# A decoder layer's last stage: a root and a scaling earlier, one addition on GpSimd, sixteen transposes half a product later

## The chip, the cores and the metric

The kernel runs on one core of a Trainium2 chip. The metric is the device time of one execution in microseconds. TensorE multiplies matrices, VectorE, ScalarE and GpSimd work on elements, and SyncE (and ScalarE) issue the transfers. The engines run their own instruction lists and meet at semaphores.

## The reference, cut to what matters

One layer over 1024 tokens of width 1024, all in float32: an RMS norm, one input projection to 8720 columns, a sliding-window attention (16 heads) and an mLSTM (8 heads) side by side, a projection of each branch, a gated merge, an output projection with the residual, and a final RMS norm.

```
branch_a = (attn * silu(a_z)) @ w_branch_attn
h_m      = sigmoid(m_o) * head_rms_norm(h_tilde) * silu(m_z)
branch_m = h_m @ w_branch_mlstm
merged   = sigmoid(g_attn) * branch_a + sigmoid(g_mlstm) * branch_m
y        = x + merged @ w_out
out      = y * rsqrt(mean(y * y, axis=-1) + 1e-6) * final_norm_w
```

## The kernel before, in words

Large products are done block-wise with seven half-size products in place of eight (Winograd's form of Strassen's method). A "pair" is such a group of seven; its order on TensorE is 1, 6, 2, 7, 4, 5, 3, and product n is done when `p<n>_done` rises. Each float32 operand is split into a high and a low part, so one product is 4 blocks times 3 terms, 12 matmuls of 128x128 by 128x512 (`PRODUCT` is 12, `PAIR` 84). A product starts only when the low part of its weights is there (`w<n>_ready`). These low parts and the weight sums are made by GpSimd, in an order written out by hand; the high parts are made by ScalarE.

The pairs 0 to 31 are the input projection, with the attention and the mLSTM woven between. Pairs 32 to 35 (`WPAIRS` + a) are the attention branch's projection. The mLSTM's last two heads are finished under them: VectorE scales their values (`normalised_h`, L2841, gives `m_h`), TensorE transposes them (`turn_h`, L1450 to L1456, 16 transposes, gives `m_h_turned`), and VectorE gates them (`gated_h`, after product 4 of pair 33). VectorE starts L2841 only when GpSimd has made the low part for product 2 of pair 33. GpSimd's list for that pair (`second_branch_pair`, L964) is: first sum, low 1, second sum, low 6, third sum, low 2, fourth sum, low 7, low 3, low 4, low 5. TensorE waits for `w7_ready` at the first matmul of product 7 (L1230). In the kernel before, `turn_h` stands between product 2 and product 7 of pair 33.

Then come the mLSTM branch's projection, the merge, and the output projection in four pairs (o = 0 to 3, `output_pair`, L1566), each for two tiles of 128 tokens. In the last pair the quarters are called c11, c21 (first and second half of the columns of tile 6) and c12, c22 (those of tile 7; the views in code are `y_part(o, j, h)`, j the tile and h the half). VectorE combines the products' banks and the residual x into them. ScalarE squares each quarter and sums (`square`, L2272, `res_sumsq`), VectorE makes the variance (`variances`, L2977 on), ScalarE the root (`res_root`), VectorE the reciprocal (`res_var`). The last pair's product 3 is done in two halves of the columns, so that c12 comes in two halves as well. The final gain is multiplied in by GpSimd (`weighted`, L1068, `sum_made`) for c11, c21 and c22, and by VectorE for c12. Before the change c21 is scaled half by VectorE (L3090) and half by ScalarE (L2343), c11 by VectorE, c22 by ScalarE. SyncE issues four of the last five stores in the order c21, c11, first part of c22, c12 (L800 to L808), and ScalarE issues the other part of c22.

Of the kernel before, what the change touches and what calls it, by code (L numbers as in the profile page):

```python
# [8 lines left out]
ALU = mybir.AluOpType  # L9
# [118 lines left out]
def build(nc, x, norm_w, w_in, b_in, sinks, conv_w, conv_b, mnorm_w, wba, wbm, w_out, fnorm_w, out):  # L128
    ctx = ExitStack()
    with ctx:  # L130
# [449 lines left out]
        def _(sp):  # L580
# [213 lines left out]
            for o in range(1, OPAIRS):  # L794
                store_tiles((0, 1, 2, 3)[o])
                if o < OPAIRS - 1:
                    for j in range(2):
                        sp.wait_ge((c21_out, c22_out)[j], SPAIRS + o + 1)
                        sp.dma_start(x_more[:, j, :], x_rows[:, 2 * o + j + 2, :]).then_inc(x_in[2 * o + j + 2], 16)
            sp.wait_ge(res_root, OPAIRS + 1)  # L800
            sp.wait_ge(y_ready, NB - 1)
            sp.dma_start(out_part(NB - 2, 1, True), y_part(OPAIRS - 1, 0, 1)).then_inc(y_out[0], 16)
            sp.wait_ge(y_ready, NB)
            sp.dma_start(out_part(NB - 2, 0, True), y_part(OPAIRS - 1, 0, 0)).then_inc(y_out[0], 16)
            sp.wait_ge(res_root, OPAIRS + 3)
            sp.dma_start(out_part(NB - 1, 1, True)[:, 0, :], y_part(OPAIRS - 1, 1, 1)[:, 0, :]).then_inc(y_out[1], 16)
            sp.wait_ge(y_ready, NB + 1)
            sp.dma_start(out_part(NB - 1, 0, True), y_part(OPAIRS - 1, 1, 0)).then_inc(y_out[1], 16)  # L808

            for s in range(2):  # L810
# [8 lines left out]
        def _(pool):  # L819
# [253 lines left out]
            pool.wait_ge(p4_done, SPAIRS + OPAIRS)  # L1073
            pool.wait_ge(res_sumsq, 4 * OPAIRS - 3)
            weighted(0, 0)
            for j in range(2):
                pool.wait_ge(res_sumsq, 4 * OPAIRS - 2 + j)
                weighted(j, 1)
# [3 lines left out]
        def _(pe):  # L1082
# [421 lines left out]
            for a in range(BPAIRS):  # L1504
                if a == 0:
                    first_branch_pair(WPAIRS)
                elif a == 1:
                    pairs(WPAIRS + 1, 0, 3 * PRODUCT)
                    turn_h(PAIRS - 1)
                    pairs(WPAIRS + 1, 3 * PRODUCT, PAIR)  # L1510
                else:
                    pairs(WPAIRS + a, 0, PAIR)

# [110 lines left out]
        def _(act):  # L1624
# [668 lines left out]
            for o in range(OPAIRS):  # L2293
                last = o == OPAIRS - 1
                if o == 0:
                    o_high_7(0)
                    o_high_3(0)
                    again_high(0, o_s1)
                if o > 1:
                    o_head(o)  # L2300
                o_high_5(o)
                if o == 0:
                    again_high(1, o_s4)
                    o_high_1(1)
                else:
                    act.wait_ge(res_var, o)
                    A(roots(o - 1, 2), roots(o - 1, 2), ACT.Sqrt).then_inc(res_root, 1)
                if not last:
                    o_high_2(o + 1)
                if o:  # L2310
                    act.wait_ge(res_sumsq, 4 * o)
                square(o, c11_out, 0, 0)
                if o and not last:
                    o_high_1(o + 1)
                if not last:
                    o_high_7(o + 1)
                    o_high_6(o + 1)
                if o == 0:
                    o_high_3(1)
                    o_head(1)  # L2320
                act.wait_ge(res_sumsq, 4 * o + 1)
                square(o, c21_out, 0, 1)
                act.wait_ge(res_sumsq, 4 * o + 2)
                square(o, c22_out, 1, 1)
                if last:
                    act.wait_ge(res_var, OPAIRS)
                    A(rstd[:, 0:1], rstd[:, 0:1], ACT.Sqrt).then_inc(res_root, 1)
                if o and not last:
                    o_high_3(o + 1)
                act.wait_ge(res_sumsq, 4 * o + 3)  # L2330
                if not last:
                    square(o, c12_out, 1, 0)
                else:

                    for a in range(2):
                        act.wait_ge(c12_out, SPAIRS + OPAIRS + a)
                        A(squares[:, 2 * P * a:2 * P * a + 2 * P], y_part(o, 1, 0)[:, a, :], ACT.Square,
                          accum_out=sumsq[:, 2 + 2 * a:3 + 2 * a]).then_inc(res_sumsq, 1)
                        if a == 0:
                            act.wait_ge(res_var, OPAIRS + 1)  # L2340
                            act.wait_ge(sum_made, 4 * (SPAIRS + OPAIRS) + 2)
                            c21 = y_part(o, 0, 1)[:, 1, :]
                            A(c21, c21, ACT.Copy, scale=rstd[:, 0:1]).then_inc(res_root, 1)  # L2343

            act.wait_ge(res_var, OPAIRS + 2)
            act.wait_ge(res_sumsq, 4 * OPAIRS + 1)
            A(rstd[:, 1:2], sumsq[:, 4:5], ACT.Sqrt, scale=1.0 / D, bias=rstd[:, 2:3]).then_inc(res_root, 1)
            act.wait_ge(res_var, OPAIRS + 3)
            act.wait_ge(sum_made, 4 * (SPAIRS + OPAIRS) + 3)
            last_half = y_part(OPAIRS - 1, 1, 1)  # L2350
            for a in range(2):
                A(last_half[:, a, :], last_half[:, a, :], ACT.Copy, scale=rstd[:, 1:2]).then_inc(res_root, 1)
# [5 lines left out]
        def _(dve):  # L2358
# [649 lines left out]
            for o in range(OPAIRS):  # L3008
# [45 lines left out]
                    o_head(1)  # L3054
                dve.wait_ge(x_in[2 * o + 1], 16 * 2)
                V.tensor_tensor(c22, c22, x_part(o, 1, 1), ALU.add)
                V.tensor_tensor(c12, c12, x_part(o, 1, 0), ALU.add)
                if not last:
                    o_low_7(o + 1)
                dve.drain()  # L3060
                dve.wait_ge(p5_done, i + 1)
                half_of(bank_b, c22, c22).then_inc(c22_out, 1)
                half_of(bank_b, c12, c12)
                if last:
                    variances(o, 1)
                dve.drain()
                if not last:
                    dve.wait_ge(p3_done, i + 1)
                    half_of(bank_c, c12, c12).then_inc(c12_out, 1)
                else:  # L3070
                    for a in range(2):
                        dve.wait_ge(p3_done, i + 1 + a)
                        V.scalar_tensor_tensor(c12[:, a, :], ps[:, (bank_c, bank_a)[a], 2 * P * a:2 * P * a + 2 * P], 0.5,
                                               c12[:, a, :], ALU.mult, ALU.add).then_inc(c12_out, 1)
                        if a == 0:
                            dve.wait_ge(res_root, OPAIRS)
                            V.reciprocal(rstd[:, 0:1], rstd[:, 0:1]).then_inc(res_var, 1)
                            dve.wait_ge(res_sumsq, 4 * OPAIRS - 1)
                            V.tensor_scalar(rstd[:, 2:3], sumsq[:, 3:4], 1.0 / D, EPS, ALU.mult, ALU.add)
                if not last:  # L3080
# [1 line left out]


            fnw_2 = fnw[:].rearrange("p (a n) -> p a n", a=4)[:, 0:2, :]
            c11, c21, c12 = y_part(OPAIRS - 1, 0, 0), y_part(OPAIRS - 1, 0, 1), y_part(OPAIRS - 1, 1, 0)
            dve.drain()
            dve.wait_ge(res_sumsq, 4 * OPAIRS)
            V.scalar_tensor_tensor(rstd[:, 2:3], sumsq[:, 2:3], 1.0 / D, rstd[:, 2:3], ALU.mult, ALU.add).then_inc(res_var, 1)
            dve.wait_ge(sum_made, 4 * (SPAIRS + OPAIRS) + 2)
            V.tensor_scalar(c21[:, 0, :], c21[:, 0, :], rstd[:, 0:1], None, ALU.mult).then_inc(y_ready, 1)  # L3090
            V.tensor_scalar(c11, c11, rstd[:, 0:1], None, ALU.mult).then_inc(y_ready, 1)
            dve.wait_ge(res_root, OPAIRS + 2)
            V.reciprocal(rstd[:, 1:2], rstd[:, 1:2]).then_inc(res_var, 1)
# [25 lines left out]
```

## Time and profile before

| what | value |
|---|---|
| median of 3 runs | 1060.74 us (1060.45 to 1060.93) |
| the profiled execution | 1060.53 us, of it span 1058.8 us |
| TensorE | busy 1047.3 us, 99% of the span |
| VectorE, ScalarE, GpSimd | 776.0, 536.5, 681.4 us |
| last matmul starts | 1052.08 us |
| the last tile's root starts (ScalarE L2347) | 1054.12 us |
| last store issued (ScalarE L2354) | 1055.58 us |

Times within the execution count from the start of the span. The span ends when the last store is known to have landed. A busy matmul row overlaps the next: the distance of their starts is the time that one costs.

### The profile page before, as it was taken

The page shows a single profiled execution, that of the slowest core. Times are in us where ns is not written, and L with a number is a line of the kernel's source. Part 1 is how long each engine was busy: PE and PEld are TensorE (multiplying, and loading weights), DVE is VectorE, ACT ScalarE, POOL GpSimd, SP SyncE. Part 2 cuts the span into 40 slices and gives each one's busy share as a digit, 9 for nine tenths or more (in the row PEclk, how much of TensorE's full clock was granted, in tenths as well). Part 3 has the DMA queues.
Part 4 walks back from the last instruction along what each step waited for, and adds up shares of the span by engine and source line. Part 5 has one row for each costly group of instructions (what it writes and reads, how often), then busy time and mean ns, then how long its engine had stood idle before and what let it go on. Part 6 is the DMA issues. An engine that isn't in the chain of part 4 may idle for free.

```text
span 1058.8 us, 18865 instructions
## 1 busy us (share of the span) xinstructions
PE 1047.3 (99%) x6415; PEld 853.7 (81%) x6415; DVE 776.0 (73%) x1199; ACT 536.5 (51%) x1279; POOL 681.4 (64%) x468
## 2 busy tenths in 40 slices
PE   8999999999999999999999999999999999999997
PEld 7887788888888888888878888888778788888886
DVE  5964785776777967767776686768688847766897
ACT  7544655655656643555345454545466444113543
POOL 4577555565565568668956797569858994545442
PEclk9999999999999999999999999999999999999999
DMA  6225132242242232314313423233329539766324
GB/s 224 74 92 91 41 120 61 61 123 76 59 120 71 81 120 80 95 47 150 119 42 90 130 89 99 89 119 90 91 80 363 173 131 332 252 249 256 162 100 139
DMA packets 122094, 131.80 MB, mean 124 GB/s; under 512 B 7900, under 2 KB 97304, under 8 KB 120488
## 3 DMA queue, kind: packets, MB, share of 16 engines
q1 hardware_dynamic: 107464, 85.60, 26.5%
q10 hardware_dynamic: 14560, 45.29, 12.9%
q8 instruction: 41, 0.67, 0.3%
q14 instruction: 29, 0.24, 0.1%
HBM read 96.16 MB, written 34.70 MB: 124 GB/s over the span
## 4 chain that ended last, share of the span: by engine, by line
PE 94%; DVE 2%; DMA 1%; ACT 1%; POOL 1%; DVEq 0%; issue 0%; POOLq 0%; ACTq 0%
PE ps L1198 68%; PE ps L1541 8%; PE ps L1103 4%; PE ps L1311 2%; PE ps L1291 2%; PE ps L1367 2%; PE ps L1439 1%; PE ps L1421 1%; PE ps L1436 1%; PE ps L1433 1%; PE ps L1150 1%; PE ps L1454 1%; PE ps L1387 1%; PE ps L1426 1%; POOL ring_lo L863 1%; DMA w<-in_w_branch_attn 1%
## 5 line engine op out<-in xcount | busy, mean ns | idle before, releaser
L863 POOL TENSOR_TENSOR ring_lo<-w,ring_hi 128x512 fp32r<-128x512 f32 x142 | 207.7, 1481 | 101.1 <-ACT ring_hi L1679 101.1
L863 POOL TENSOR_TENSOR ring_lo<-t,ring_hi 128x512 fp32r<-128x512 f32 x108 | 155.6, 1446 | 125.1 <-ACT ring_hi L1679 125.0
L1198 PE MATMUL ps<-s_hi,ring_hi 128*128 128x512 f32 x560 | 221.5, 396 | 0.0
L1198 PE MATMUL ps<-s_lo,ring_hi 128*128 128x512 f32 x560 | 219.3, 392 | 0.0
L1198 PE MATMUL ps<-s_hi,ring_lo 128*128 128x512 f32 x560 | 219.1, 391 | 0.0
L1198 PE MATMUL ps<-h_hi,ring_hi 128*128 128x512 f32 x420 | 165.5, 394 | 0.3 <-DVE merged L2464 0.3
L1198 PE MATMUL ps<-h_lo,ring_hi 128*128 128x512 f32 x420 | 163.7, 390 | 0.0
L1198 PE MATMUL ps<-h_hi,ring_lo 128*128 128x512 f32 x420 | 163.7, 390 | 0.0
L1679 ACT ACTIVATE ring_hi<-w 128x512 fp32r<-128x512 f32 x144 | 86.7, 622 | 100.8 <-PE ps L1198 95.7
L1198 PEld LDWEIGHTS ps<-s_hi,ring_lo 128*128 128x128 f32 x560 | 105.1, 188 | 21.5
L1198 PEld LDWEIGHTS ps<-s_hi,ring_hi 128*128 128x128 f32 x560 | 105.2, 188 | 21.2 <-POOL ring_lo L863 0.4
L1198 PEld LDWEIGHTS ps<-s_lo,ring_hi 128*128 128x128 f32 x560 | 105.3, 188 | 20.6 <-issue 0.3
L858 POOL TENSOR_TENSOR t<-w,t 128x512 f32<-128x512 f32 x72 | 107.4, 1492 | 8.1 <-issue 5.1
L1679 ACT ACTIVATE ring_hi<-t 128x512 fp32r<-128x512 f32 x108 | 67.3, 625 | 65.5 <-PE ps L1198 52.6
L1198 PEld LDWEIGHTS ps<-h_hi,ring_hi 128*128 128x128 f32 x420 | 79.1, 188 | 16.7 <-POOL ring_lo L863 1.0
L1198 PEld LDWEIGHTS ps<-h_hi,ring_lo 128*128 128x128 f32 x420 | 78.8, 188 | 16.5
L1198 PEld LDWEIGHTS ps<-h_lo,ring_hi 128*128 128x128 f32 x420 | 78.9, 188 | 15.6
L1541 PE MATMUL ps<-u_m,w_hi 128*128 128x512 f32 x256 | 78.8, 389 | 0.0
L1906 ACT ACTIVATE probs<-probs,neg_max 128x128 f32<-128x128 f32 x128 | 49.8, 390 | 34.7 <-DVE sink_in L2574 34.5
L858 POOL TENSOR_TENSOR t<-w,w 128x512 f32<-128x512 f32 x36 | 56.2, 1561 | 16.2 <-issue 8.1
L1541 PEld LDWEIGHTS ps<-u_m,w_hi 128*128 128x128 f32 x256 | 48.0, 188 | 10.1
L858 POOL TENSOR_TENSOR w<-w,w 128x512 f32<-128x512 f32 x36 | 50.4, 1401 | 0.0
(336 smaller groups left out, 2085.2 us busy)
## 6 DMA issues: line engine op xcount, KB each, us to landing
w<-in_w_in SPq DMA_DIRECT2D x128, 256.0 KB, 3.1
xs<-in_x SPq DMA_DIRECT2D x8, 512.0 KB, 7.4
ga_scratch<-ev ACTq DMA_DIRECT2D x4, 1024.0 KB, 4.8
c_rows<-c_scratch ACTq DMA_DIRECT2D x8, 512.0 KB, 6.5
ev<-u_scratch SPq DMA_DIRECT2D x8, 512.0 KB, 5.0
u_sums_scratch<-ev ACTq DMA_DIRECT2D x4, 1024.0 KB, 5.0
m_scratch<-mz ACTq DMA_DIRECT2D x4, 1024.0 KB, 4.0
w<-in_w_branch_attn SPq DMA_DIRECT2D x16, 256.0 KB, 3.7
```

Source lines behind the costliest of these rows:

```text
L858: return nc.gpsimd.tensor_tensor(flat(dst), flat(a), flat(b), op)
L863: return nc.gpsimd.tensor_tensor(flat(lo[:]), flat(raw_or_sum[:]), flat(hi[:]).bitcast(F32), ALU.subtract)
L1103: mm = nc.tensor.matmul(ps[:, 2 * s + b, :], w[:, k, :], h[:, k % KH, :], start=(r == 0), stop=(r == KT * TERMS - 1))
L1150: mm = nc.tensor.matmul(ps[:, 2 * slot(GATES) + b, :], w_hi[GATES][:, k, :], H[b][k // KH][m % 2][:, k % KH, :], start=(m == 0), stop=(m = ...
L1198: mm = nc.tensor.matmul(ps[:, bank, columns], w[:, k, :], h[:, k, columns], start=(m == 0), stop=(m == PRODUCT - 1))
L1291: mm = nc.tensor.matmul(ps[64 * half:64 * half + 64, SCORES[r], column:column + keys], q_T[rows, j, queries], k_now[rows, first:first + keys],
L1311: mm = nc.tensor.matmul(pv_ps(slice(64 * r, 64 * r + 64), half), v_m, pT[rows, 2 * r:2 * r + 2, queries], start=start, stop=stop)
L1367: mm = nc.tensor.transpose(ps[:, TURNED, h * P:(h + 1) * P], probs[n % 2][:, h, :], ident[:])
L1387: mm = nc.tensor.transpose(ps[:, X[2 * j + c // 4], (c % 4) * P:(c % 4 + 1) * P], ev[:, j, c * P:(c + 1) * P], ident[:])
L1541: mm = nc.tensor.matmul(ps[:, 2 * s + b, :], w[:, k, :], part(k)[(0, 1, 0)[term]][:, token_half(b)], start=starts, stop=stops)
L1679: return A(ring_slot[0][:], raw_or_sum[:], ACT.Copy)
L1906: A(pr[:, h, :], pr[:, h, :], ACT.Exp, scale=HD ** -0.5, bias=neg_max[:, h:h + 1], accum_out=row_sum[:, h:h + 1])
```

## The change

There are two parts.

In the last output pair: VectorE no longer adds x to c12; GpSimd does, in a new `tensor_tensor` that waits for `c21_out` and stands between the weighting of c11 and that of c21. VectorE makes tile 6's variance directly after adding x to c22 (before: after both additions of the bank). Its reciprocal follows the bank's addition to c22. ScalarE takes tile 6's root ahead of the squares of c22, and scales the whole of c21 ahead of the squares of c12 (before: its second half, between them; the first half was scaled by VectorE). VectorE waits for GpSimd's addition before it adds the bank to c12. SyncE waits for ScalarE's semaphore before c21's store.

In pair 33: `turn_h` moves from between products 2 and 7 to the middle of product 7, six matmuls later.

```diff
--- before.py
+++ after.py
@@ -798,13 +798,13 @@
                         sp.wait_ge((c21_out, c22_out)[j], SPAIRS + o + 1)
                         sp.dma_start(x_more[:, j, :], x_rows[:, 2 * o + j + 2, :]).then_inc(x_in[2 * o + j + 2], 16)
             sp.wait_ge(res_root, OPAIRS + 1)
+            sp.wait_ge(res_root, OPAIRS + 1)
+            sp.dma_start(out_part(NB - 2, 1, True), y_part(OPAIRS - 1, 0, 1)).then_inc(y_out[0], 16)
             sp.wait_ge(y_ready, NB - 1)
-            sp.dma_start(out_part(NB - 2, 1, True), y_part(OPAIRS - 1, 0, 1)).then_inc(y_out[0], 16)
-            sp.wait_ge(y_ready, NB)
             sp.dma_start(out_part(NB - 2, 0, True), y_part(OPAIRS - 1, 0, 0)).then_inc(y_out[0], 16)
             sp.wait_ge(res_root, OPAIRS + 3)
             sp.dma_start(out_part(NB - 1, 1, True)[:, 0, :], y_part(OPAIRS - 1, 1, 1)[:, 0, :]).then_inc(y_out[1], 16)
-            sp.wait_ge(y_ready, NB + 1)
+            sp.wait_ge(y_ready, NB)
             sp.dma_start(out_part(NB - 1, 0, True), y_part(OPAIRS - 1, 1, 0)).then_inc(y_out[1], 16)
 
             for s in range(2):
@@ -1073,6 +1073,10 @@
             pool.wait_ge(p4_done, SPAIRS + OPAIRS)
             pool.wait_ge(res_sumsq, 4 * OPAIRS - 3)
             weighted(0, 0)
+            c12 = y_part(OPAIRS - 1, 1, 0)
+            pool.wait_ge(x_in[NB - 1], 16 * 2)
+            pool.wait_ge(c21_out, SPAIRS + OPAIRS)
+            nc.gpsimd.tensor_tensor(c12, c12, x_part(OPAIRS - 1, 1, 0), ALU.add).then_inc(sum_made, 1)
             for j in range(2):
                 pool.wait_ge(res_sumsq, 4 * OPAIRS - 2 + j)
                 weighted(j, 1)
@@ -1505,9 +1509,9 @@
                 if a == 0:
                     first_branch_pair(WPAIRS)
                 elif a == 1:
-                    pairs(WPAIRS + 1, 0, 3 * PRODUCT)
+                    pairs(WPAIRS + 1, 0, 3 * PRODUCT + PRODUCT // 2)
                     turn_h(PAIRS - 1)
-                    pairs(WPAIRS + 1, 3 * PRODUCT, PAIR)
+                    pairs(WPAIRS + 1, 3 * PRODUCT + PRODUCT // 2, PAIR)
                 else:
                     pairs(WPAIRS + a, 0, PAIR)
 
@@ -2320,11 +2324,11 @@
                     o_head(1)
                 act.wait_ge(res_sumsq, 4 * o + 1)
                 square(o, c21_out, 0, 1)
-                act.wait_ge(res_sumsq, 4 * o + 2)
-                square(o, c22_out, 1, 1)
                 if last:
                     act.wait_ge(res_var, OPAIRS)
                     A(rstd[:, 0:1], rstd[:, 0:1], ACT.Sqrt).then_inc(res_root, 1)
+                act.wait_ge(res_sumsq, 4 * o + 2)
+                square(o, c22_out, 1, 1)
                 if o and not last:
                     o_high_3(o + 1)
                 act.wait_ge(res_sumsq, 4 * o + 3)
@@ -2332,21 +2336,20 @@
                     square(o, c12_out, 1, 0)
                 else:
 
+                    act.wait_ge(res_var, OPAIRS + 1)
+                    act.wait_ge(sum_made, 4 * (SPAIRS + OPAIRS) + 3)
+                    c21 = y_part(o, 0, 1)
+                    A(c21, c21, ACT.Copy, scale=rstd[:, 0:1]).then_inc(res_root, 1)
                     for a in range(2):
                         act.wait_ge(c12_out, SPAIRS + OPAIRS + a)
                         A(squares[:, 2 * P * a:2 * P * a + 2 * P], y_part(o, 1, 0)[:, a, :], ACT.Square,
                           accum_out=sumsq[:, 2 + 2 * a:3 + 2 * a]).then_inc(res_sumsq, 1)
-                        if a == 0:
-                            act.wait_ge(res_var, OPAIRS + 1)
-                            act.wait_ge(sum_made, 4 * (SPAIRS + OPAIRS) + 2)
-                            c21 = y_part(o, 0, 1)[:, 1, :]
-                            A(c21, c21, ACT.Copy, scale=rstd[:, 0:1]).then_inc(res_root, 1)
 
             act.wait_ge(res_var, OPAIRS + 2)
             act.wait_ge(res_sumsq, 4 * OPAIRS + 1)
             A(rstd[:, 1:2], sumsq[:, 4:5], ACT.Sqrt, scale=1.0 / D, bias=rstd[:, 2:3]).then_inc(res_root, 1)
             act.wait_ge(res_var, OPAIRS + 3)
-            act.wait_ge(sum_made, 4 * (SPAIRS + OPAIRS) + 3)
+            act.wait_ge(sum_made, 4 * (SPAIRS + OPAIRS) + 4)
             last_half = y_part(OPAIRS - 1, 1, 1)
             for a in range(2):
                 A(last_half[:, a, :], last_half[:, a, :], ACT.Copy, scale=rstd[:, 1:2]).then_inc(res_root, 1)
@@ -3054,15 +3057,19 @@
                     o_head(1)
                 dve.wait_ge(x_in[2 * o + 1], 16 * 2)
                 V.tensor_tensor(c22, c22, x_part(o, 1, 1), ALU.add)
-                V.tensor_tensor(c12, c12, x_part(o, 1, 0), ALU.add)
                 if not last:
+                    V.tensor_tensor(c12, c12, x_part(o, 1, 0), ALU.add)
                     o_low_7(o + 1)
+                else:
+                    variances(o, 1)
                 dve.drain()
                 dve.wait_ge(p5_done, i + 1)
                 half_of(bank_b, c22, c22).then_inc(c22_out, 1)
+                if last:
+                    dve.wait_ge(res_root, OPAIRS)
+                    V.reciprocal(rstd[:, 0:1], rstd[:, 0:1]).then_inc(res_var, 1)
+                    dve.wait_ge(sum_made, 4 * (SPAIRS + OPAIRS) + 2)
                 half_of(bank_b, c12, c12)
-                if last:
-                    variances(o, 1)
                 dve.drain()
                 if not last:
                     dve.wait_ge(p3_done, i + 1)
@@ -3073,8 +3080,6 @@
                         V.scalar_tensor_tensor(c12[:, a, :], ps[:, (bank_c, bank_a)[a], 2 * P * a:2 * P * a + 2 * P], 0.5,
                                                c12[:, a, :], ALU.mult, ALU.add).then_inc(c12_out, 1)
                         if a == 0:
-                            dve.wait_ge(res_root, OPAIRS)
-                            V.reciprocal(rstd[:, 0:1], rstd[:, 0:1]).then_inc(res_var, 1)
                             dve.wait_ge(res_sumsq, 4 * OPAIRS - 1)
                             V.tensor_scalar(rstd[:, 2:3], sumsq[:, 3:4], 1.0 / D, EPS, ALU.mult, ALU.add)
                 if not last:
@@ -3082,12 +3087,10 @@
 
 
             fnw_2 = fnw[:].rearrange("p (a n) -> p a n", a=4)[:, 0:2, :]
-            c11, c21, c12 = y_part(OPAIRS - 1, 0, 0), y_part(OPAIRS - 1, 0, 1), y_part(OPAIRS - 1, 1, 0)
+            c11, c12 = y_part(OPAIRS - 1, 0, 0), y_part(OPAIRS - 1, 1, 0)
             dve.drain()
             dve.wait_ge(res_sumsq, 4 * OPAIRS)
             V.scalar_tensor_tensor(rstd[:, 2:3], sumsq[:, 2:3], 1.0 / D, rstd[:, 2:3], ALU.mult, ALU.add).then_inc(res_var, 1)
-            dve.wait_ge(sum_made, 4 * (SPAIRS + OPAIRS) + 2)
-            V.tensor_scalar(c21[:, 0, :], c21[:, 0, :], rstd[:, 0:1], None, ALU.mult).then_inc(y_ready, 1)
             V.tensor_scalar(c11, c11, rstd[:, 0:1], None, ALU.mult).then_inc(y_ready, 1)
             dve.wait_ge(res_root, OPAIRS + 2)
             V.reciprocal(rstd[:, 1:2], rstd[:, 1:2]).then_inc(res_var, 1)
```

## Rows read from the trace of the kernel before

**Rows 1.** The page: busy us (share of the span) and instructions, by engine
```profile
...
PE 1047.3 (99%) x6415; PEld 853.7 (81%) x6415; DVE 776.0 (73%) x1199; ACT 536.5 (51%) x1279; POOL 681.4 (64%) x468
```

**Rows 2.** Waits of TensorE's weight loads, 842 us to the end: total, times, longest
```profile
...
PEld ps L1198 <- POOL ring_lo L863: 0.3, 1, 0.3
```

**Rows 3.** Order of time, TensorE, 836.8 to 842.9: start, us, engine, line
```profile
...
837.28 0.39 PE L1198 MATMUL ps<-h_hi,ring_lo 128*128 128x512 f32 x1
837.83 1.97 PE L1454 MATMUL ps<-ident,v 128*128 128x128 f32 x16 [0.16 <-DVE v L2841]
839.55 0.47 PE L1198 MATMUL ps<-s_hi,ring_hi 128*128 128x512 f32 x1
...
842.45 0.50 PE L1198 MATMUL ps<-h_hi,ring_hi 128*128 128x512 f32 x1
```

**Rows 4.** Order of time, VectorE, GpSimd and SyncE's queue, 834 to 839
```profile
...
834.40 3.37 DVE L2841 TENSOR_TENSOR v<-v,rstd 128x2048 f32<-128x2048 f32 x1 [2.50 <-POOL ring_lo L863]
...
835.56 3.35 POOL L863 TENSOR_TENSOR ring_lo<-w,ring_hi 128x512 fp32r<-128x512 f32 x1
...
838.94 0.37 SPq L697 DMA_DIRECT2D w<-in_w_branch_attn  x1
```

**Rows 5.** Order of time, VectorE in the tail
```profile
...
1048.37 0.69 DVE L3051 TENSOR_TENSOR merged<-merged 128x512 f32<-128x512 f32 x1
1049.15 0.69 DVE L3056 TENSOR_TENSOR merged<-merged,x_more 128x512 f32<-128x512 f32 x1
...
1050.52 1.29 DVE L2975 SCALAR_TENSOR_TENSOR merged<-ps,merged 128x512 f32<-128x512 f32 x2
1051.73 0.15 DVE L2982 TENSOR_TENSOR rstd<-sumsq 128x1 f32<-128x1 f32 x1
...
1054.45 0.16 DVE L3093 RECIPROCAL rstd<-rstd 128x1 f32<-128x1 f32 x1 [0.37 <-ACT rstd L2347]
```

**Rows 6.** Order of time, ScalarE in the last 23 us
```profile
...
1038.19 1.15 ACT L2216 ACTIVATE o_ring_hi<-o_t 128x512 fp32r<-128x512 f32 x2
...
1053.14 0.49 ACT L2343 ACTIVATE merged<-merged,rstd 128x256 f32<-128x256 f32 x1
1053.54 0.40 ACT L2337 ACTIVATE squares<-merged 128x256 f32<-128x256 f32 x1
...
1054.12 0.29 ACT L2347 ACTIVATE rstd<-sumsq,rstd 128x1 f32<-128x1 f32 x1
```

**Rows 7.** Order of time, GpSimd in the tail: c21's weighting
```profile
...
1049.95 1.65 POOL L1070 TENSOR_TENSOR merged<-merged,fnw 128x512 f32<-128x512 f32 x1 [4.12 <-ACT squares L2275]
```

**Rows 8.** GpSimd and VectorE close together; L2786: shortest, median, longest ns
```profile
...
205.78 0.16 DVE L2579 TENSOR_TENSOR row_inv<-row_sum,sink_exp 128x4 f32<-128x4 f32 x1
205.78 1.30 POOL L863 TENSOR_TENSOR ring_lo<-w,ring_hi 128x512 fp32r<-128x512 f32 x1 [5.98 <-ACT ring_hi L1679]
...
221.66 1.28 POOL L858 TENSOR_TENSOR t<-w,w 128x512 f32<-128x512 f32 x1 [0.76 <-DMA w<-in_w_in]
221.69 1.81 DVE L2596 SCALAR_TENSOR_TENSOR z_part<-z_part,silu_z 128x512 f32<-128x512 f32 x1 [0.16 <-issue]
...
1000.95 0.69 DVE L2948 TENSOR_TENSOR o_ring_lo<-o_t,o_ring_hi 128x512 fp32r<-128x512 f32 x1
...
1001.72 1.30 POOL L1026 TENSOR_TENSOR o_t<-merged 128x512 f32<-128x512 f32 x1 [5.68 <-DVE o_ring_lo L2948]
...
L2786 DVE SCALAR_TENSOR_TENSOR den<-v x32: 161/163/1314, 422.3 to 793.4; 128x2 f32<-128x2 f32 x32
```

**Rows 9.** Store issues, and two half-microseconds of the data: DMA share, GB/s
```profile
...
1053.77 0.41 SPq L802 DMA_DIRECT2D out<-merged  x1
...
1055.57 0.46 SPq L808 DMA_DIRECT2D out<-merged  x1
...
1054.50:1055.00 0.50, 0.00 (x0) 0.00 (x0) 0.40 (x2) 0.35 (x1) 0.00 (x0) 1.00 0.60 197
...
1057.50:1058.00 0.50, 0.00 (x0) 0.00 (x0) 0.00 (x0) 0.00 (x0) 0.00 (x0) 0.50 0.59 203
```


## The prediction

> **What bounds the kernel now.** I read first the busy shares and the chain: TensorE is busy 99% of the span [rows 1]. So before the last product a microsecond counts only where TensorE waits, and anything that makes it wait is paid in full unless a later wait takes it back. The waits of TensorE from 842 us to its end hold a single entry, 0.3 us in total [rows 2]; nothing there can absorb a delay. The change has two places: the transposes of the last two heads near 838 us, and the tail, where the chain leaves TensorE and runs over VectorE, ScalarE and the stores. For the first I read TensorE's order in time [rows 3] beside what its semaphores wait for [rows 4]; for the second, VectorE, ScalarE, GpSimd and the store issues of the tail [rows 5 to 7, 9], and how GpSimd and VectorE behave when both work on SBUF [rows 8].
>
> **The transposes, half a product later.** Before: product 2 issues its last matmul at 837.28; twelve go from 839.55 to 842.40, one about every 0.23 us, so the next could go at 837.51. The 16 transposes start at 837.83, because VectorE's L2841 (`m_h`) ends at 834.40+3.37 = 837.77 [rows 3, 4]. That is 0.32 us of idle, all that moving them can win. After: six matmuls of product 7 come first, and `product_7` waits for `w7_ready` before its first matmul. Who gives it? GpSimd's `low_7`, the L863 at 835.56, which takes 3.35 us and ends at 838.91; SyncE's L697, which waits for the same semaphore, issues at 838.94 and confirms it [rows 4]. Today the transposes cover that wait (product 7 starts at 839.55). With the new order TensorE stands from 837.51 to about 838.96, 1.45 us. Then the same work follows: transposes 839.55-837.83 = 1.72, product 7 12 matmuls in 842.40-839.55 = 2.85 (842.45 less the 0.05 that product 4 waits today), and product 4 starts at 838.96+4.57 = 843.53 instead of 842.45 [rows 3]. Its own low parts are there, since it could start at 842.45 today. Loss: 1.08 us, nothing later gives it back [rows 2]. The transposed values are ready 2.5 us later (842.0 instead of 839.5), but VectorE uses them only behind product 4's sum, so nobody waits. Bounds of this step: -0.32 (if `w7_ready` were early) and +1.2 (if the split of product 7 costs another restart like the 0.47 of the matmul at 839.55 against 0.39).
>
> **The tail, step by step** (times on the old clock, to which the 1.08 is added).
> SyncE: one store waits for `res_root` in place of `y_ready`; same five stores, same order, no instruction more. Nothing.
> VectorE loses `c12 += x` (L3057) and L3090; L3090 lay beside ScalarE's work. ScalarE scales all of c21 (512 columns) ahead of the last squares, where it did 256 between them: 0.40 us from start to start for 256 (1053.14 to 1053.54) [rows 6]; two passes of 512 took 1.15 together, at most 0.57 each [rows 6], and I take 0.54 for 512. GpSimd gets one 128x512 addition; behind it in its queue stand c21's and c22's weighting, for both of which ScalarE waits.
> The addition starts on `c21_out`, given by L3051, which ends at 1048.37+0.69 = 1049.06. GpSimd starts 0.08 us after a VectorE semaphore (1000.95+0.69 = 1001.64, then 1001.72) [rows 8]: 1049.14. VectorE's own next step, `c22 += x` L3056, starts at 1049.15 [rows 5]. Both read two operands from SBUF. Started 0.03 us behind GpSimd, such a VectorE operation took 1.81 us (221.69), to 0.56 past GpSimd's end; at a dead heat (205.78) it was let through, and of eight such pairs within 0.01 us four were let through and four took 1.3 us; even a 128x2 operation, normally 163 ns, had 1314 [rows 8]. The other way round GpSimd pays: L1070 at 1049.95 took 1.65 us beside L3057, ending 1.15 after it [rows 7]. With a lag of 0.01 to 0.02 I give GpSimd the first place by 6 to 4. The Trainium skill, "SBUF — State Buffer", section "Who interferes with whom", says that a two-input VectorE instruction and a GpSimd one that reads SBUF exclude each other and that issue order decides who blocks; the trace agrees, and by issue order GpSimd is first.
>
> GpSimd first: it works 1049.14 to 1050.43. L3056 ends at 1050.43+0.55 = 1050.98 (was 1049.84). GpSimd's next, c21's weighting, has its release since 1049.95 [rows 7] and has stood in line, so it goes then, to 1050.98+1.15 = 1052.13. The new `variances` on VectorE begins with a two-input operation, 128x1: it waits to 1052.16. (Uncontended the pair costs 0.47 from start to next start, 1051.73 to 1052.20; the second has one input.) Then: second half of the variance to 1052.39; `c22 += bank` 1052.48 to 1053.17; reciprocal; `c12 += bank` 1053.15 to 1053.84; first half of the last tile 1053.93 to 1054.36 and the second half from 1054.33 [rows 5]. ScalarE: square of c22 1053.26 (0.57 and 0.07 for its sum), c21 scaled 1053.90, squares of the last tile 1054.44 and 1054.85, root 1055.43 where it was 1054.12 [rows 6]: +1.31. VectorE's scaling of c11 now ends at 1055.93, 0.1 us later than the root's reciprocal wants, so the reciprocal comes at 1055.86 where it was 1054.45 [rows 5]: +1.41, and the last issues with it.
> The stores: first issue 1053.77, last 1055.57 [rows 9]. Data flow from about 1054.7 (0.95 after the first issue) to 1057.8 without a gap at about 342 GB/s, 1.05 MB in 3.07 us [rows 9]. The last store and the 128 KB ScalarE one beside it, 393 KB, need 1.15 us. Last issue 1055.57+1.41 = 1056.98, +0.95+1.15 = 1059.08 against 1057.79: **+1.3**. Today's end is limited by the stream, not by the last issue (1055.57+2.10 = 1057.67), hence 0.1 less than the issues slip.
>
> Sum: 1060.53 (the profiled execution; span 1058.8 and 1.7 around it) +1.08 +1.3 = 1062.9. The median of the runs is 0.21 above the profiled one: **1063.1 us**.
>
> **Rivals.**
> A: VectorE wins the heat. L3056 ends at 1049.84, GpSimd's addition at 1050.99, the 128x1 operation waits for it to 1051.02, `c22 += bank` starts at 1051.34 (was 1050.52), the root at 1054.3 (+0.2), the last issues +0.26, the data +0.14. Total +1.2: 1062.0. For it: half of the dead heats. Against: the lag of 0.01 to 0.02.
> B: the 128x1 operation is not held up (no row shows this form beside GpSimd; 128x2 is the nearest). Then the tail gives +0.3 with GpSimd first, and with VectorE first the intended gain: `c22 += bank` at 1050.4, root at 1053.86, data end 0.35 earlier. Totals +1.4 and +0.7: 1062.1 and 1061.5.
> C, the other side, not slower than before: the transposes' move costs nothing. Mechanism: `w7_ready` at 837.5 or earlier, that is `low_7` in its uncontended 1.3 us (835.56 to 836.85), if L2841 did not hold it off. Then TensorE wins 0.32 us there, and with the tail's -0.35 the kernel comes to 1060.1; with the tail's +1.3, 1061.7. It decides from the point where GpSimd's L863 ends before 837.5. Against: L2841 starts when `low_2` ends, at 834.4, and `low_7` follows only at 835.56, behind fourth_sum, so VectorE has always claimed first; nothing in the change touches either.
> D: the tail's lateness hides because the stream of stores is the bound. It would need the last issue to slip less than 0.1 us; no case above does.
>
> **Numbers.** Forecast (both costs) 0.47; A 0.30; B 0.13; C 0.10. A measurement tells about 0.2%, 2.1 us, from no change: 1058.6 to 1062.9. The forecast lies 0.2 us past that edge, and an error of 0.25 us in either stage is likely, so I count four fifths of it, plus a little of A and B with a longer wait, as slower: 0.42. Faster by 2.1 us has no mechanism: 0.02. The rest, 0.56, within. Range: A and B from below, with the low end of C's slower half, 1061.0; above, the forecast plus 0.6 for another GpSimd turn in between: 1063.7.
>
> **What would show it.** Step 1: TensorE idle of about 1.4 us before product 7 of the second branch pair, released by GpSimd's L863, and product 4 about 1.1 us later against product 2's end; wrong if the transposes' wait just vanishes. Step 2: `c22 += x` at 1.8 us beside GpSimd's addition at 1.3 (forecast), or 0.69 beside 1.8 (A). Step 3: the 128x1 operation of `variances` above 1 us; 0.15 is B. Step 4: the last tile's root starts about 6.4 us after `c21 += c22` ends (before: 1054.12-1049.06 = 5.1). Step 5: data from the first store no longer flow without a gap. The forecast is wrong if the sum of steps 1 and 4 is under 1.5 us.

## The result, and the profile after

The changed kernel takes 1062.60 us (median of 22 runs, 1061.91 to 1065.58), the kernel before 1060.93 us in its 22 runs beside it (1060.18 to 1062.03). The ratio of the two is 1.0017, 95% interval 1.0011 to 1.0023: slower by about 1.7 us. The profiled execution took 1062.66 us with a span of 1060.6.

The page's head (span, then busy time, share and instructions by engine): all of the loss is idle time, TensorE's busy time is the same within 0.2 us.

```profile
span 1060.6 us, 18864 instructions
...
PE 1047.5 (99%) x6415; PEld 853.5 (80%) x6415; DVE 777.4 (73%) x1197; ACT 536.6 (51%) x1279; POOL 683.5 (64%) x469
```

TensorE around the transposes, in order of time (start, us, engine, line, operation; in brackets the idle time before it and who ended it). These answer to [rows 3].

```profile
...
837.79 0.39 PE L1202 MATMUL ps<-h_hi,ring_lo 128*128 128x512 f32 x1
839.49 0.50 PE L1202 MATMUL ps<-s_hi,ring_hi 128*128 128x512 f32 x1 [1.30 <-POOL ring_lo L863]
...
840.98 1.91 PE L1458 MATMUL ps<-ident,v 128*128 128x128 f32 x16
842.64 0.47 PE L1202 MATMUL ps<-s_hi,ring_hi 128*128 128x512 f32 x1
...
844.11 0.40 PE L1202 MATMUL ps<-h_hi,ring_hi 128*128 128x512 f32 x1
```

VectorE's scaling of the values and GpSimd's low 7 there, answering to [rows 4].

```profile
...
834.93 3.37 DVE L2844 TENSOR_TENSOR v<-v,rstd 128x2048 f32<-128x2048 f32 x1 [2.50 <-POOL ring_lo L863]
```

```profile
...
836.10 3.33 POOL L863 TENSOR_TENSOR ring_lo<-w,ring_hi 128x512 fp32r<-128x512 f32 x1
```

The reader is to see three things. The six matmuls of product 7 go first now, and the first of them (839.49) waits 1.30 us for GpSimd. That GpSimd row is `low_7`, 3.33 us long (before 3.35), since VectorE's scaling, which began first, holds it off until 834.93+3.37 = 838.30. And from the last start of product 2 to the first of product 4 it is 844.11-837.79 = 6.32 us, against 842.45-837.28 = 5.17 [rows 3]: 1.15 us lost. From 842 us to the end the trace has no wait of TensorE.

VectorE in the tail, answering to [rows 5] (line 3054 was 3051, 3059 was 3056, 2985 was 2982).

```profile
...
1049.90 0.69 DVE L3054 TENSOR_TENSOR merged<-merged 128x512 f32<-128x512 f32 x1
1050.69 0.69 DVE L3059 TENSOR_TENSOR merged<-merged,x_more 128x512 f32<-128x512 f32 x1
1051.44 1.10 DVE L2985 TENSOR_TENSOR rstd<-sumsq 128x1 f32<-128x1 f32 x1
1052.63 0.15 DVE L2987 TENSOR_SCALAR rstd<-rstd 128x1 f32<-128x1 f32 x1
1052.87 0.69 DVE L2978 SCALAR_TENSOR_TENSOR merged<-ps,merged 128x512 f32<-128x512 f32 x1
...
1056.35 0.16 DVE L3096 RECIPROCAL rstd<-rstd 128x1 f32<-128x1 f32 x1 [0.21 <-ACT rstd L2350]
```

GpSimd there: the new addition (line 1079) and c21's weighting, which was [rows 7].

```profile
...
1050.74 1.79 POOL L1079 TENSOR_TENSOR merged<-merged,x_more 128x512 f32<-128x512 f32 x1 [3.37 <-DVE merged L3054]
1052.50 1.29 POOL L1070 TENSOR_TENSOR merged<-merged,fnw 128x512 f32<-128x512 f32 x1
```

ScalarE: the scaling of all of c21, the two squares, the last tile's root; [rows 6].

```profile
...
1054.41 0.72 ACT L2342 ACTIVATE merged<-merged,rstd 128x512 f32<-128x512 f32 x1
1055.04 0.40 ACT L2345 ACTIVATE squares<-merged 128x256 f32<-128x256 f32 x1
...
1055.44 0.40 ACT L2345 ACTIVATE squares<-merged 128x256 f32<-128x256 f32 x1
...
1056.03 0.29 ACT L2350 ACTIVATE rstd<-sumsq,rstd 128x1 f32<-128x1 f32 x1
```

SyncE's first and last of the last stores, and three stretches of the data (DMA share, GB/s last); [rows 9].

```profile
...
1055.21 0.41 SPq L802 DMA_DIRECT2D out<-merged  x1
...
1057.47 0.46 SPq L808 DMA_DIRECT2D out<-merged  x1
...
1057.00:1057.50 0.50, 0.00 (x0) 0.00 (x0) 0.37 (x1) 0.46 (x2) 0.00 (x0) 1.00 0.76 260
1057.50:1058.00 0.50, 0.00 (x0) 0.00 (x0) 0.00 (x0) 0.00 (x0) 0.00 (x0) 0.91 0.86 289
...
1059.50:1060.00 0.50, 0.00 (x0) 0.00 (x0) 0.00 (x0) 0.00 (x0) 0.00 (x0) 0.50 0.15 47
```

`c22 += x` keeps its 0.69 us and GpSimd's addition takes 1.79: VectorE came first. But `variances`' first operation, 128x1, takes 1.10 where it took 0.15, and the bank's addition to c22 starts 2.97 us after `c21 += c22` (before 2.15). The root starts 1056.03-1049.90 = 6.13 us after it, against 5.75. The data no longer flow at the full rate throughout (a share of 0.76 in one half-microsecond; before, 0.98 or more in each from 1055.0 to 1057.5). The table shows the tail in us, all counted from the start of `c21 += c22`; the names are those of the experiments below.

| run | last tile's root | ScalarE's store issued | span's end |
|---|---|---|---|
| before | 5.75 | 7.21 | 10.4 |
| changed | 6.13 | 7.59 | 10.7 |
| tail only | 6.12 | 7.58 | 10.7 |
| one input | 5.61 | 7.08 | 10.2 |
| two small operations | 7.32 | 8.78 | 11.8 |
| one wait | 7.26 | 8.72 | 11.8 |
| c11 first | 5.60 | 7.07 | 10.3 |
| no two inputs | 5.24 | 6.88 | 10.2 |

Of the 1.8 us between the two spans, 1.15 lie in the transposes, 0.3 in the tail, and 0.5 had arisen before product 2's end (837.79 against 837.28) in code that the change does not touch; from product 4 to the tail 0.1 came back. In the twelve other profiled executions that point lay between 837.16 and 838.18, and at 837.27 and 837.52 in two of one and the same kernel (c11 first), so this is spread between executions.

### The profile page after: what moved, and what is told of

It is laid out like the page before. It is cut to its first block, busy times and chain, and to the rows that moved or that the text cites. A ratio compares the mean times of both kernels' runs of the same rounds, so it can differ in the third digit from the quotient of the medians.

```text
span 1060.6 us, 18864 instructions
## 1 busy us (share of the span) xinstructions
PE 1047.5 (99%) x6415; PEld 853.5 (80%) x6415; DVE 777.4 (73%) x1197; ACT 536.6 (51%) x1279; POOL 683.5 (64%) x469
## 4 chain that ended last, share of the span: by engine, by line
PE 94%; DVE 2%; POOL 1%; DMA 1%; ACT 1%; DVEq 0%; POOLq 0%; issue 0%; SPq 0%; ACTq 0%
PE ps L1202 68%; PE ps L1545 8%; PE ps L1107 4%; PE ps L1315 2%; PE ps L1295 2%; PE ps L1371 2%; PE ps L1443 1%; PE ps L1425 1%; POOL ring_lo L863 1%; PE ps L1440 1%; PE ps L1437 1%; PE ps L1154 1%; PE ps L1391 1%; PE ps L1458 1%; PE ps L1430 1%; DMA xs<-in_x 1%
```

## The experiments

Each run was timed in five rounds beside the kernel before. The intervals of single runs are about 0.9 us wide on each side, so medians a few tenths apart tell nothing alone; there the readings below rest on one trace of each run.

**1. The tail alone** (`e1`): the changed kernel with the transposes put back.

```diff
-                    pairs(WPAIRS + 1, 0, 3 * PRODUCT + PRODUCT // 2)
+                    pairs(WPAIRS + 1, 0, 3 * PRODUCT)
                     turn_h(PAIRS - 1)
-                    pairs(WPAIRS + 1, 3 * PRODUCT + PRODUCT // 2, PAIR)
+                    pairs(WPAIRS + 1, 3 * PRODUCT, PAIR)
```

> The changed kernel with the 16 transposes back between products 2 and 7; only the tail's edits are left. Theory (two separate costs: 1.1 us for TensorE's wait for w7_ready, 0.3 us in the tail): 0.2 to 0.5 us above the kernel before, TensorE's wait at 839 us gone, the tail as in the changed kernel: variances' 128x1 operation at 1.1 us, from the start of c21 += c22 to the last tile's root 6.1 us (before 5.75). Rival (the tail holds most of the loss): 1.3 us or more above the kernel before.

1061.20 us against 1060.65, ratio 1.0003 (0.9994 to 1.0012). The tail is the changed kernel's to 0.01 us (table), as expected, and it costs 0.3 us in the trace and by the ratio (0.55 by the medians).

**2. The transposes alone** (`e2`): the kernel before with the opposite of that diff.

> The kernel before with only the transposes moved half a product later. Theory: TensorE stands 1.3 to 1.5 us for GpSimd's low 7 and the kernel is 1.0 to 1.3 us slower than before. Rival (the loss is the tail's): within 0.3 us of the kernel before.

1061.46 us against 1060.65, ratio 1.0011 (1.0002 to 1.0020). TensorE, in order of time:

```profile
...
837.19 0.39 PE L1198 MATMUL ps<-h_hi,ring_lo 128*128 128x512 f32 x1
838.87 0.50 PE L1198 MATMUL ps<-s_hi,ring_hi 128*128 128x512 f32 x1 [1.29 <-POOL ring_lo L863]
...
843.50 0.40 PE L1198 MATMUL ps<-h_hi,ring_hi 128*128 128x512 f32 x1
```

843.50-837.19 = 6.31 us: the loss of the changed kernel to 0.01 us, with the same wait (1.29 us) for GpSimd. The ratio gives 1.2 us, within the 1.0 to 1.3 expected; the medians give 0.8.

**3. GpSimd's order turned round** (`e3`): the second run, and in `second_branch_pair`

```diff
                 low_2(i)
-                fourth_sum(i)
                 low_7(i)
+                fourth_sum(i)
```

> The kernel before with the transposes moved, and in GpSimd's list for that pair low 7 in front of the fourth sum, so that w7_ready comes near 835.6 us, before VectorE takes SBUF for the heads' values. Theory (the wait for w7_ready is the whole cost of the move): no wait before product 7; the gain of 0.3 us that is then open is held back by w4_ready, since the fourth sum now waits for VectorE and low 4 still ends near 842.4; the kernel is within 0.3 us of the kernel before. Rival (splitting product 7, or the later transposes, cost by themselves): still 1 us slower than before.

1060.77 us against 1060.65, ratio 1.0002 (0.9993 to 1.0011). TensorE, then GpSimd:

```profile
...
837.22 0.39 PE L1198 MATMUL ps<-h_hi,ring_lo 128*128 128x512 f32 x1
837.45 0.39 PE L1198 MATMUL ps<-s_hi,ring_hi 128*128 128x512 f32 x1
...
842.38 0.50 PE L1198 MATMUL ps<-h_hi,ring_hi 128*128 128x512 f32 x1 [0.26 <-POOL ring_lo L863]
```

```profile
...
833.00 2.54 POOL L863 TENSOR_TENSOR ring_lo<-w,ring_hi 128x512 fp32r<-128x512 f32 x2
835.50 3.34 POOL L858 TENSOR_TENSOR t<-w,t 128x512 f32<-128x512 f32 x1
```

Low 2 and low 7 now run back to back from 833.00 to 835.54, and product 7 starts at 837.45, 0.23 us after product 2's last matmul: no wait. It is the fourth sum that waits for VectorE (3.34 us). From product 2 to product 4: 5.16 us, as before the change, because product 4 waits 0.26 us for its own low part. So the move of the transposes cost only what `w7_ready` cost, and the 0.3 us it was to win goes to the next wait.

**4. One tensor input** (`e4`): the first run, and in `variances`

```diff
-                V.tensor_tensor(r, halves[:, :, 0], halves[:, :, 1], ALU.add)
+                if tiles == 1:
+                    V.tensor_scalar(r, sumsq[:, 0:1], sumsq[:, 1:2], None, ALU.add)
+                else:
+                    V.tensor_tensor(r, halves[:, :, 0], halves[:, :, 1], ALU.add)
```

> The tail's edits alone (as the run of the tail alone), with the first operation of tile 6's variance written as an operation with one tensor input and a per-partition scalar in place of two tensor inputs; the result is the same sum. Theory (two SBUF tensor inputs make VectorE wait for GpSimd's addition even at 128x1): it falls from 1.1 to 0.15 us, the bank's addition to c22 starts about 1 us earlier, the last tile's root comes 0.6 to 0.9 us earlier, and the kernel is 0.4 to 0.8 us faster than the tail alone, 0.1 to 0.5 us faster than before. Rival (it waits for something else, such as the sum of squares or a drain): no difference from the tail alone.

1060.76 us against 1060.65, ratio 1.0002 (0.9993 to 1.0011): 0.44 below the tail alone by the medians, 0.1 by the ratios, which no interval tells from nothing. The 0.1 to 0.5 us that it was to be faster than before did not show. VectorE, then ScalarE:

```profile
...
1048.79 0.69 DVE L3057 TENSOR_TENSOR merged<-merged 128x512 f32<-128x512 f32 x1
...
1050.33 0.21 DVE L2986 TENSOR_SCALAR rstd<-sumsq 128x1 f32<-128x1 f32 x1
...
1050.87 0.69 DVE L2978 SCALAR_TENSOR_TENSOR merged<-ps,merged 128x512 f32<-128x512 f32 x1
```

```profile
...
1052.79 0.72 ACT L2342 ACTIVATE merged<-merged,rstd 128x512 f32<-128x512 f32 x1 [0.42 <-POOL merged L1070]
...
1054.40 0.29 ACT L2350 ACTIVATE rstd<-sumsq,rstd 128x1 f32<-128x1 f32 x1
```

The operation takes 0.21 us instead of 1.10, with the same addition running on GpSimd (1.79 us); the bank's addition starts 2.08 us after `c21 += c22` instead of 2.97. The root comes 0.5 us earlier, not 0.6 to 0.9: ScalarE now waits 0.42 us for GpSimd's weighting of c21, the next in line.

**5. Two small operations** (`e5`) and **6. one wait** (`e6`), both on the first run, are two ways to make GpSimd come first: VectorE 0.15 us later by two 128x1 reciprocals of unused columns, or GpSimd earlier.

```diff
+                if last:
+                    V.reciprocal(rstd[:, 8:9], rstd[:, 8:9])
+                    V.reciprocal(rstd[:, 9:10], rstd[:, 9:10])
                 V.tensor_tensor(c22, c22, x_part(o, 1, 1), ALU.add)
```

```diff
+            pool.wait_ge(x_in[NB - 1], 16 * 2)
             pool.wait_ge(p4_done, SPAIRS + OPAIRS)
             pool.wait_ge(res_sumsq, 4 * OPAIRS - 3)
             weighted(0, 0)
             c12 = y_part(OPAIRS - 1, 1, 0)
-            pool.wait_ge(x_in[NB - 1], 16 * 2)
             pool.wait_ge(c21_out, SPAIRS + OPAIRS)
```

> The tail alone, with two 128x1 reciprocals on unused columns put in front of VectorE's c22 += x, so that it starts about 0.15 us later, after GpSimd's addition. Theory (whoever starts first holds the SBUF reads for its whole instruction): c22 += x takes about 1.7 us, GpSimd's addition 1.3; then the weighting of c21 is served before the 128x1 operation of variances, which takes more than 1 us; the last tile's root comes 1.0 to 1.4 us later than in the tail alone and the kernel is 0.9 to 1.3 us slower than the tail alone. Rival (they share the reads and nothing depends on order): 0.15 us slower than the tail alone.

> The tail alone, with GpSimd's wait for the last x tile moved ahead of its first weighting, so that only the wait for c21_out stands directly before the addition. Theory (the second wait cost GpSimd its place: in the changed kernel it starts 0.15 us after VectorE's c21 addition ends, against 0.08 elsewhere): GpSimd's addition starts within 0.02 us of c22 += x; either VectorE still wins and nothing changes, or GpSimd wins and the kernel is 0.9 to 1.3 us slower. Rival (GpSimd's start does not depend on its number of waits): start 0.15 us after, no change.

1062.55 and 1062.50 us against 1060.91, ratios 1.0015 (1.0006 to 1.0024) and 1.0013 (1.0004 to 1.0022). VectorE, then GpSimd's addition, of the fifth run:

```profile
...
1050.21 1.75 DVE L3062 TENSOR_TENSOR merged<-merged,x_more 128x512 f32<-128x512 f32 x1
1051.89 1.25 DVE L2985 TENSOR_TENSOR rstd<-sumsq 128x1 f32<-128x1 f32 x1
```

```profile
...
1050.13 1.29 POOL L1079 TENSOR_TENSOR merged<-merged,x_more 128x512 f32<-128x512 f32 x1 [3.37 <-DVE merged L3054]
```

VectorE, GpSimd and ScalarE's root of the sixth:

```profile
...
1048.27 0.69 DVE L3054 TENSOR_TENSOR merged<-merged 128x512 f32<-128x512 f32 x1
1049.06 1.83 DVE L3059 TENSOR_TENSOR merged<-merged,x_more 128x512 f32<-128x512 f32 x1
1050.81 1.24 DVE L2985 TENSOR_TENSOR rstd<-sumsq 128x1 f32<-128x1 f32 x1
...
1052.38 0.69 DVE L2978 SCALAR_TENSOR_TENSOR merged<-ps,merged 128x512 f32<-128x512 f32 x1
```

```profile
...
1049.04 1.30 POOL L1079 TENSOR_TENSOR merged<-merged,x_more 128x512 f32<-128x512 f32 x1 [3.31 <-DVE merged L3054]
1050.30 1.74 POOL L1070 TENSOR_TENSOR merged<-merged,fnw 128x512 f32<-128x512 f32 x1
```

```profile
...
1055.53 0.29 ACT L2350 ACTIVATE rstd<-sumsq,rstd 128x1 f32<-128x1 f32 x1
```

With one wait in front of it GpSimd starts 0.08 us after `c21 += c22` ends (1048.27+0.69 = 1048.96), with two it was 0.15. Why a wait for data that were loaded long before (their transfers were issued by 1036 us, and such a load lands about 3.4 us later) should cost that is not shown. The start is now 0.02 us before `c22 += x`, and the roles turn: VectorE 1.83, GpSimd 1.30; then GpSimd's weighting, which stood in line, is served before the 128x1 operation (1.24). The root comes at 7.26 instead of 6.12, the span's end 1.1 us later. These are the steps of the forecast's tail, brought about by taking a wait forward.

**7. Both repairs and low 4 first** (`e7`) and **8. both repairs** (`e8`): the changed kernel with the edits of runs 3 and 4; the seventh also has

```diff
                 fourth_sum(i)
-                low_3(i)
                 low_4(i)
+                low_3(i)
                 low_5(i)
```

> The changed kernel with three repairs: low 7 in front of the fourth sum, low 4 in front of low 3 (so that product 4 is not held back), and the one-input form of the variance. Theory: no wait of TensorE from 836 us on, product 4 starts 4.6 us after product 2's last matmul starts plus 0.23 (before: 5.17), 0.3 us won there and 0.2 in the tail: 0.3 to 0.6 us faster than before. Rival (moving low 4 only shifts the wait to product 5 or to the next pair's weights): within 0.2 us of before, with a wait for GpSimd further on.

> The changed kernel with low 7 in front of the fourth sum and the one-input form of the variance. Theory (these two waits are the whole loss): 1.3 to 1.9 us faster than the changed kernel, 0.0 to 0.4 us faster than before. Rival (a part of the changed kernel's loss of 1.7 us has another cause, since the two parts alone gave only 0.55 and 0.8): still 0.3 us or more slower than before.

The eighth: 1060.95 us against 1060.91, ratio 1.0001 (0.9992 to 1.0010). The whole loss is gone, but nothing that can be told is gained over the kernel before (0.0 to 0.4 us was expected; the trace shows 5.14 us from product 2 to product 4, tail 10.2). The seventh: 1062.41, ratio 1.0015 (1.0006 to 1.0024), a miss: 0.3 to 0.6 us faster was expected. Its product 4 does start 4.72 us after product 2's last matmul, 0.45 sooner than before. But here is TensorE ten microseconds later, and what led to it (SyncE's issue, then GpSimd's second sum and low 1 of the next pair):

```profile
...
852.12 0.50 PE L1202 MATMUL ps<-h_hi,ring_hi 128*128 128x512 f32 x1 [1.48 <-POOL ring_lo L863]
```

```profile
...
843.59 0.37 SPq L701 DMA_DIRECT2D w<-in_w_branch_attn  x1
...
848.29 1.29 POOL L858 TENSOR_TENSOR t<-w,t 128x512 f32<-128x512 f32 x1 [1.95 <-DMA w<-in_w_branch_attn]
...
850.79 1.27 POOL L863 TENSOR_TENSOR ring_lo<-w,ring_hi 128x512 fp32r<-128x512 f32 x1
```

SyncE loads the next pair's `w22` when low 3 is done: at 843.59, where the kernel before issued that load at 840.18. The second sum waits 1.95 us for it. Low 1 stands behind that sum and the third in GpSimd's list and ends at 850.79+1.27 = 852.06, and product 1 of the next pair waits 1.48 us for it. The first part of the rival had it, the wait was only shifted; but it came back larger than it left.

**9. c11 first** (`e9`, run again as `e12`) and **11. no two inputs** (`e11`): the fourth run, and ScalarE scales c11 at once, SyncE stores it first, and VectorE scales c21 near the end. VectorE's first step of the last tile's variance also moves behind the second half of c12 (`if a == 0` becomes `if a == 1`; this and SyncE's lines are left out below).

```diff
                     A(rstd[:, 0:1], rstd[:, 0:1], ACT.Sqrt).then_inc(res_root, 1)
+                    act.wait_ge(res_var, OPAIRS + 1)
+                    act.wait_ge(sum_made, 4 * (SPAIRS + OPAIRS) + 1)
+                    c11 = y_part(o, 0, 0)
+                    A(c11, c11, ACT.Copy, scale=rstd[:, 0:1]).then_inc(res_root, 1)
...
-                    c21 = y_part(o, 0, 1)
-                    A(c21, c21, ACT.Copy, scale=rstd[:, 0:1]).then_inc(res_root, 1)
...
-            V.tensor_scalar(c11, c11, rstd[:, 0:1], None, ALU.mult).then_inc(y_ready, 1)
+            dve.wait_ge(sum_made, 4 * (SPAIRS + OPAIRS) + 3)
+            V.tensor_scalar(c21, c21, rstd[:, 0:1], None, ALU.mult).then_inc(y_ready, 1)
```

and in the eleventh, besides:

```diff
-            V.scalar_tensor_tensor(rstd[:, 2:3], sumsq[:, 2:3], 1.0 / D, rstd[:, 2:3], ALU.mult, ALU.add).then_inc(res_var, 1)
+            V.tensor_scalar(rstd[:, 2:3], sumsq[:, 2:3], 1.0 / D, rstd[:, 2:3], ALU.mult, ALU.add).then_inc(res_var, 1)
```

> The kernel before, with the tail's edits in the one-input form and one more: ScalarE scales c11 (whose weighting is long done) right after tile 6's reciprocal and SyncE stores it first, and VectorE scales c21 after the last tile's halves, so that ScalarE's last squares wait for no weighting by GpSimd. Theory (in the one-input run ScalarE waited 0.4 us for GpSimd's weighting of c21 and then spent 0.6 us on it ahead of the last squares): the last squares start with c12's halves, the last tile's root comes 0.4 to 0.6 us earlier against c21's addition than in the one-input run, 5.1 us after its start, the last store is issued as much earlier, and the kernel is 0.3 to 0.7 us faster than before. Rival (the stores are one stream of 3.1 us and its first byte counts, or the weighting by GpSimd stays in the way on VectorE): within 0.2 us of before.

> The run that stores c11 first, with the last 128x1 operation of the last tile's variance, which took 0.78 us beside GpSimd's weighting of c22, also written with one tensor input and a per-partition scalar. Theory (each two-input VectorE operation beside GpSimd's works through that whole addition or multiplication, however small): it takes 0.2 us, the last tile's root starts 5.1 to 5.2 us after c21's addition starts (before 5.75, c11-first 5.60), the last store is issued 0.4 us earlier than in the c11-first run, and the kernel is 0.3 to 0.6 us faster than that run, 0.2 to 0.6 us faster than before. Rival (the 0.45 us of ScalarE's wait there came from the sum of squares, not from GpSimd): no change against the c11-first run.

> The c11-first run again, on the same chip as the run with no two-input operation, so that the two can be compared: 0.2 us faster to 0.3 us slower than before by both theories, since only its neighbour differs.

c11 first: 1060.93 against 1060.50, ratio 1.0005 (0.9995 to 1.0014), and again 1061.04 against 1060.85, ratio 0.9999 (0.9990 to 1.0008). No gain, where 0.3 to 0.7 us was expected: the last squares did start on time, but the last tile's 128x1 operation now lay beside GpSimd's weighting of c22. That row, then the same place (and c21's scaling behind it) in the eleventh run:

```profile
...
1053.09 0.78 DVE L3096 SCALAR_TENSOR_TENSOR rstd<-sumsq,rstd 128x1 f32<-128x1 f32 x1 [0.28 <-ACT squares L2345]
```

```profile
...
1053.04 0.21 DVE L3096 TENSOR_SCALAR rstd<-sumsq,rstd 128x1 f32<-128x1 f32 x1 [0.27 <-ACT squares L2345]
1053.16 0.92 DVE L3098 TENSOR_SCALAR merged<-merged,rstd 128x512 f32<-128x512 f32 x1
```

0.78 us with two tensor inputs, 0.21 with one, and the root comes at 5.24 instead of 5.60 (expected 5.1 to 5.2). The eleventh takes 1060.80 us against 1060.85, ratio 0.9999 (0.9990 to 1.0008); 0.2 to 0.6 us faster was expected. The span's end is 0.2 to 0.3 us earlier than before the change in its trace, half of the 0.5 us that the root gained: c21's scaling, 512 columns on VectorE, took 0.92 us beside GpSimd (0.47 in c11 first, where it began only 0.07 us before GpSimd's end). So its store was issued at 1054.11, and the data then flow almost without a gap to the end (shares of 0.90 to 1.03 from 1055.0 to 1057.0). No version found here beats the kernel before by an amount that can be measured.

**10. The changed kernel again** (`e10`).

> The changed kernel as it is, in the same job, to see whether its two parts add up. Theory (two independent costs, 0.55 us measured for the tail alone and 0.81 for the transposes alone): 1.3 to 1.7 us slower than before. Rival (a third cost that shows only when both are there): 2 us or more.

1062.58 us against 1060.50, ratio 1.0016 (1.0007 to 1.0025); by the medians 2.1 us, the rival's figure, by the ratio 1.7, the theory's. The parts alone gave 0.55 and 0.81 by medians, 0.3 and 1.15 by their traces. In this trace both stages are as in the parts alone to 0.01 us (6.32 us from product 2 to product 4, root at 6.12), and the two repairs together bring the kernel back, so no third cost is needed; with intervals of this width an interplay of half a microsecond elsewhere can't be excluded.

## Why the prediction was right or wrong

- **The transposes.** Right in every step. Idle 1.45 us expected at product 7, 1.3 found (839.49 instead of an unhindered 838.02, 1.47 us from start to start); loss 1.08 expected, 1.15 found. The rest is about one more restart (the first matmul after a pause or after the transposes holds TensorE 0.32 us, later ones 0.23), which the bounds had. Run 3 shows the cause, and rival C's mechanism with it: once `w7_ready` is early the cost is gone. C's gain of 0.32 did not come, because product 4's low part is next; the prediction had read that wait of today as 0.05 us and did not carry it into C.
- **The order of the two additions.** Wrong, and this is the step of the forecast that failed. It put GpSimd first at 6 to 4, by a start 0.08 us after the semaphore. That 0.08 was read from a row with one wait before it; the new addition has two, started 0.15 after, and so came 0.05 us behind VectorE (run 6 moves one wait away and gets 0.08). Rival A happened: the tail cost 0.3 us, not 1.3.
- **The 128x1 operation.** Right, in the changed kernel and in run 4: 1.10 us against 0.15 to 0.21. No row of before showed this form beside GpSimd; the 128x2 row was the right neighbour [rows 8]. Run 4 puts it down to the second tensor input: only the form changed. Rival B falls.
- **The sizes.** For A the bank's addition to c22 was put 0.82 us later, found 0.82. The root was put 0.2 later, found 0.38: c21's scaling holds ScalarE 0.63 us from start to start, not 0.54, and the square of c22 before it with the reading of its sum 0.75, not 0.64. The data's end was put 0.14 later, and the span's end came 0.3 later.
- **The forecast's own tail**, +1.3 us, is about what runs 5 and 6 show when GpSimd is first: the span's end 11.8 instead of 10.4 us after `c21 += c22`.
- **The time.** 1063.1 was forecast, with A at 1062.0; 1062.6 was measured against a before of 1060.93, 0.19 above the median that the sum started from. The measured loss of 1.7 us lies between A's 1.2 and the forecast's 2.4; the two traces account for 1.3 of it from product 2's end on (run 10's for 1.4), and the rest is open. The range held both ways the tail could go, so that the time fell into it says nothing for the forecast's tail; that it lies as near to 1063.1 as to A's 1062.0 is luck.
- **Its own sign of being wrong** was a sum of steps 1 and 4 under 1.5 us. The sum is 1.15+0.38 = 1.53, just above, though the tail went the other way: A with its true sizes reaches that edge too, so the sign could not tell the two apart. Step 2's rows do.
- **Rival D** falls: the last issue slipped 0.38 us and the end 0.3 with it.

## What to carry to other kernels

Before work is moved behind a wait, look up what the moved work was covering: the 16 transposes hid 1.3 us of waiting for a weight's low part, which showed up in no list of waits. Where VectorE and GpSimd run side by side, give the small operations on the path one tensor input (a per-partition scalar takes the other). And don't let a GpSimd operation start within a tenth of a microsecond of a two-input VectorE one: a lead of 0.05 us for VectorE or of 0.02 for GpSimd decided which of them paid, and here it was worth 1.1 us. And free a wait only after following what the freed engine's next output feeds: moving one GpSimd step back by 3.4 us starved a load for the next pair.

## What the runs showed of the hardware

A VectorE operation with two SBUF tensor inputs that came while a GpSimd operation with two SBUF inputs was running waited for its end, even with one element per partition (1.10, 1.24, 1.25 and 0.78 us; alone 0.15). With one tensor input and a scalar from SBUF the 128x1 operation did not (0.21 us in all six runs that have that form). This is shown for 128x1 alone: a 128x512 scaling with one tensor input took 0.92 us beside GpSimd in run 11, against 0.47. A 128x1 operation with two inputs also gave way to a GpSimd operation that had stood in line longer (runs 5 and 6). A second wait in front of GpSimd's addition went with a start 0.07 us later (0.15 against 0.08 after the semaphore).
